# Two-layer decoder trunk on one core: the experts' products from a split operand over 128 tokens to plain fp32 over groups of 32 tokens

## What is computed

```python
def swiglu(xn, w_gu, w_down):
    gate, up = jnp.split(xn @ w_gu, 2, axis=-1)
    return (jax.nn.silu(gate) * up) @ w_down

def moe_swiglu(xn, w_router, w_gu, w_down):
    logits = (xn @ w_router).astype(jnp.float32)
    vals, idx = lax.top_k(logits, TOP_K)
    wts = jax.nn.softmax(vals, axis=-1)
    combine = jnp.sum(jax.nn.one_hot(idx, N_EXPERTS, dtype=jnp.float32) * wts[..., None], axis=-2).astype(xn.dtype)
    out = jnp.zeros_like(xn)
    for e in range(N_EXPERTS):
        out = out + combine[..., e:e + 1] * swiglu(xn, w_gu[e], w_down[e])
    return out
```

## Time and profile before

| | |
|---|---|
| runs | 1526.94, 1527.23, 1527.39 us |
| span of the profiled execution, first to last instruction | 1525.5 us (1.7 under the median; its own time is not listed) |
| TensorE busy | 1492.0 us, 98% |
| VectorE, ScalarE, POOL busy | 1187.4, 986.0, 57.1 us |
| DMA, mean over the span | 299 GB/s, 455.57 MB |
| bytes read from memory | 434.89 MB |

### The profile page before, as it was taken

How to read it: one execution, slowest core, us unless ns; L and a number is a source line. 1 busy time by engine, 2 the same in 40 slices (tenths; PEclk the granted TensorE clock), 3 DMA queues, 4 the chain that set the end, 5 groups by cost and what they waited for, 6 DMA issues and landing times.

```text
span 1525.5 us, 20065 instructions
## 1 busy us (share of the span) xinstructions
PE 1492.0 (98%) x7081; PEld 1214.1 (80%) x7081; DVE 1187.4 (78%) x1047; ACT 986.0 (65%) x1001; POOL 57.1 (4%) x83
## 2 busy tenths in 40 slices
PE   7999999999999989999999999999999999999998
PEld 6888788887776568888888888888888888888886
DVE  1489655545658558898888889889888889888997
ACT  4645444444525527778777778778778778778774
POOL 2000100000111010000000000000000000000100
PEclk9999999999999989999999999999999999999999
DMA  9333585448638039999999999999999999999994
GB/s 363 130 111 111 185 257 180 178 166 220 217 138 290 15 110 374 369 363 386 394 367 377 394 378 363 393 391 355 395 376 362 395 385 357 393 392 356 397 392 169
DMA packets 213026, 455.57 MB, mean 299 GB/s; under 512 B 9857, under 2 KB 36522, under 8 KB 212970
## 3 DMA queue, kind: packets, MB, share of 16 engines
q1 hardware_dynamic: 206624, 441.48, 79.8%
q0 software_dynamic: 3536, 12.96, 2.1%
q10 hardware_dynamic: 2810, 0.40, 0.2%
HBM read 434.89 MB, written 19.92 MB: 298 GB/s over the span
## 4 chain that ended last, share of the span: by engine, by line
PE 94%; DVE 4%; POOL 1%; issue 1%; ACT 0%; DMA 0%; DVEq 0%; POOLq 0%; ACTq 0%
PE bank L2354 60%; PE bank L1947 8%; PE bank L1964 4%; PE bank L1817 4%; PE bank L1858 3%; PE bank L2033 2%; PE bank L2209 2%; PE bank L1839 2%; PE bank L2374 2%; PE bank L1891 1%; PE bank L2103 1%; PE bank L2067 1%; DVE small L1517 1%; PE bank L2151 1%; PE bank L2178 1%
## 5 line engine op out<-in xcount | busy, mean ns | idle before, releaser
L1676 DVE TENSOR_TENSOR w_lo<-ring,w_hi 128x2048 fp32r<-128x2048 f32 x333 | 756.4, 2290 | 104.6 <-ACT w_hi L1027 104.0
L1027 ACT ACTIVATE w_hi<-ring 128x2048 fp32r<-128x2048 f32 x333 | 638.0, 1920 | 168.8 <-PE bank L2354 168.6
L2354 PE MATMUL bank<-w_hi,x_hi 128*128 128x512 f32 x896 | 244.3, 394 | 0.7 <-DVE x_lo L1684 0.7
L2354 PE MATMUL bank<-w_hi,x_lo 128*128 128x512 f32 x896 | 240.0, 390 | 0.0
L2354 PE MATMUL bank<-w_lo,x_hi 128*128 128x512 f32 x896 | 239.7, 389 | 0.0
L2354 PEld LDWEIGHTS bank<-w_hi,x_lo 128*128 128x128 f32 x896 | 168.2, 188 | 35.9
L2354 PEld LDWEIGHTS bank<-w_lo,x_hi 128*128 128x128 f32 x896 | 168.2, 188 | 35.2
L2354 PEld LDWEIGHTS bank<-w_hi,x_hi 128*128 128x128 f32 x896 | 164.5, 188 | 32.3 <-issue 0.9
L1241 DVE TENSOR_TENSOR ring_lo<-ring,f_whi 128x1024 fp32r<-128x1024 f32 x66 | 80.6, 1225 | 75.5 <-ACT f_whi L817 75.5
L2354 PE MATMUL bank<-w_hi,t_hi 128*128 128x512 f32 x448 | 122.6, 395 | 0.0
L2354 PE MATMUL bank<-w_hi,t_lo 128*128 128x512 f32 x448 | 121.1, 392 | 0.0
(11 more groups left out here) (307 smaller groups left out, 1596.6 us busy)
## 6 DMA issues: line engine op xcount, KB each, us to landing
ring<-in_moe_w_gu SPq DMA_DIRECT2D x224, 1024.0 KB, 7.6
ring<-in_moe_w_down SPq DMA_DIRECT2D x112, 1024.0 KB, 8.1
ring<-in_ffn_w_gu SPq DMA_DIRECT2D x22, 1024.0 KB, 8.1
ring<-in_hgrn_w_in SPq DMA_DIRECT2D x16, 1024.0 KB, 15.2
ring<-in_ffn_w_down SPq DMA_DIRECT2D x10, 1024.0 KB, 6.3
x_rows<-arena SPq DMA_DIRECT2D x2, 4096.0 KB, 20.2
ring<-in_kv_w SPq DMA_DIRECT2D x6, 1024.0 KB, 6.3
ring<-in_hgrn_w_out SPq DMA_DIRECT2D x4, 1024.0 KB, 6.3
```

Source lines behind the costliest of these rows:

```text
L1027: act.activation(w_hi[s % PARTS][:, :], raw[:, s % RAWS, :], ACT.Copy).then_inc(hi_ready, 1)
L1676: dve.tensor_tensor(w_lo[s % PARTS][:, :], raw[:, s % RAWS, :], w_hi[s % PARTS][:, :].bitcast(F32), ALU.subtract).then_inc(lo_ready, 1)
L2354: last = mm(out_, x_[k], w[:, k, 512 * b:512 * b + 512], start=start and k == 0 and n == 0, stop=stop and k == HALF // width - 1 and n == 2)
```

## The change

- Experts are computed in plain fp32, without the split: no `w_hi`, `w_lo`, no rounding and no subtraction. A product is one fp32 matmul in place of three fp32r ones.
- Tokens of an expert are cut in groups of 32. The stationary operand is 128 x 32, and four matmuls for the four quarters of the weight columns write the four blocks of 32 partitions of one bank (`block_product`, `row_product`). So a bank holds 32 tokens by 4 x 512 hidden columns.
- Experts are ordered by how many tokens they have. Eight places with 3, 2, 3, 3, 3, 3, 4, 2 groups take them: expert 0 is first, the fullest other is in place 6, the emptiest two in places 7 and 1. A token beyond its place's capacity sets the flag (`most > 0`), and 16 rounds of spill rows, each with a whole expert's weights, would follow.
- Weights come as 46 parts an expert, in phases: gate and up of hidden columns 0 to 2047 (8 + 8 parts, partition p has row 8p + k, 2048 columns, runs of 8 KB), gate and up of the remaining 1536 columns (8 + 8 parts, 6 KB), down (8 + 6 parts of two rows of 1024 values that lie together, 8 KB). There are 14 buffers in place of 7, and a part is free when TensorE has used it.
- The hidden values are transposed by VectorE, in blocks of 32 x 32 (`hidden`), as are the token rows (`turned_rows`). The results go out in rows of 1 KB quarters.
- TensorE, SP, ACT, DVE and POOL have the experts written out, no loop.
- Fewer rows are cleared in memory: 736 for the tokens in place of 2048, and two in place of 1152 for the results.

```diff
-HALF, RAWS, PARTS = ITEM // 2, 7, 3
-NCH = FFE // 512
-PER_E = 3 * NCH
-HALVES = 2 * PER_E
+HALF, RAWS = ITEM // 2, 14
...
+GROUPS = (3, 2, 3, 3, 3, 3, 4, 2)
+RANK = (0, 6, 2, 3, 4, 5, 1, 7)
+LAST = NE - 1
+BEFORE = tuple(sum(GROUPS[:p]) for p in range(NE + 1))
+CAPS = tuple(32 * g for g in GROUPS)
+BASE = tuple(32 * g for g in BEFORE[:NE])
+MAIN = 32 * BEFORE[NE]
+SPILL_G = 3
+SPILL_Y = (6, 7, 0)
+SPILL = T - min(CAPS)
+SPILLS = NE * SPILL // (32 * SPILL_G)
+ZEROS = (BASE[LAST], NE * SPILL)
+WIDE = (512, 384)
+COLS = (0, 4 * WIDE[0])
+DEEP = (WIDE[0] // 32, WIDE[1] // 32)
+PHASES = ((0, 0), (0, 1), (1, 0), (1, 1))
+FIRST = (0, 8, 16, 24, 32, 40)
+N_PART = 46
...
+        def raw(r):
+            at = (ITEM + r * HALF) % (SLOTS * ITEM)
+            return ring[:, at // ITEM, at % ITEM:at % ITEM + HALF]
+        def raw_full(r):
+            return half_full[r // 2] if r % 2 else slot_full[(r // 2 + 1) % SLOTS]
+        def part_here(n):
+            r = n % RAWS
+            before = 0 if r % 2 else 2 * len(range((r // 2 + 1) % SLOTS, I_MOE, SLOTS))
+            return raw_full(r), 16 * (before + n // RAWS + 1)
...
-            def halves_of(e, E, first, last):
-                for s in range(first, last):
-                    (_, kind, c), a = expert_items[s // 2], s % 2
...
-                    sp.dma_start(dst, src).then_inc(raw_full[s % RAWS], 16)
...
+            def weights(dst, s, e):
+                ph, n = phase_of(s)
+                if ph < 4:
+                    c, up = PHASES[ph]
+                    c0 = up * FFE + COLS[c]
+                    src = moe_w_gu[0, bass.ds(e, 1), :, c0:c0 + 4 * WIDE[c]].rearrange("o (p k) c -> p (o k) c", k=KD)
+                    return sp.dma_start(dst[:, 0:4 * WIDE[c]], src[:, n, :])
+                c = ph - 4
+                src = moe_w_down[0, bass.ds(e, 1), COLS[c]:COLS[c] + P * DEEP[c], :].rearrange(
+                    "o (p b) c -> p (o b) c", b=DEEP[c])
...
+            for n in range(NE * N_PART):
+                p, s = divmod(n, N_PART)
+                if s == 0 and p:
+                    if p == 1:
+                        sp.wait_ge(route_ready, 1)
+                    e = sp.value_load(m_exp[0:1, p:p + 1], min_val=0, max_val=NE - 1)
+                if n == 10:
+                    sp.wait_ge(res_ps, 11)
+                if n == 12:
+                    sp.wait_ge(res_ps, 12)
+                if n >= RAWS:
+                    sp.wait_ge(*part_used(n - RAWS))
+                weights(raw(n % RAWS), s, e).then_inc(raw_full(n % RAWS), 16)
...
+            def bring(r0, G):
+                for q in range(4):
+                    pool.dma_start(m_x[32 * q:32 * q + 32, 0:G, :], rows(x_rows, r0, G, q)).then_inc(x_full, 16)
...
-                    act.activation(w_hi[s % PARTS][:, :], raw[:, s % RAWS, :], ACT.Copy).then_inc(hi_ready, 1)
...
+            def gated(g, b, c, made, taken):
+                act.wait_ge(e_ps, made)
+                act.wait_ge(e_h, taken)
+                act.activation(m_sl[:, g, 0:WIDE[c]], bank[:, b, 0:WIDE[c]], ACT.Silu).then_inc(e_sl, 1)
...
-                    dve.tensor_tensor(w_lo[s % PARTS][:, :], raw[:, s % RAWS, :], w_hi[s % PARTS][:, :].bitcast(F32),
-                                      ALU.subtract).then_inc(lo_ready, 1)
...
+            def turned_rows(w, G, came):
+                dve.wait_ge(x_full, came)
+                step(dve.transpose(m_xt[:, w, 0:G, :, :], m_x[:, 0:G, :].rearrange("p g (a b) -> p g b a", b=KD)))
+                dve.tensor_tensor(m_xt[:, w, 0:G, :, :], m_xt[:, w, 0:G, :, :],
+                                  gain[:, G_ROWS:G_ROWS + KD].unsqueeze(1).unsqueeze(3).broadcast_to([P, G, KD, 32]),
+                                  ALU.mult).then_inc(xt_ready, 1)
...
+            def hidden(g, w, b, c, made, gate, turned, done):
+                dve.wait_ge(e_ps, made)
+                dve.wait_ge(e_sl, gate)
+                if turned is not None:
+                    dve.wait_ge(e_t, turned)
+                dve.tensor_tensor(m_h[:, w, 0:WIDE[c]], m_sl[:, g, 0:WIDE[c]], bank[:, b, 0:WIDE[c]],
+                                  ALU.mult).then_inc(e_h, 1)
+                dve.wait_ge(e_h, gate)
+                dve.wait_ge(y_ps, done)
+                dve.transpose(m_t[c][:, g, :, :],
+                              m_h[:, w, 0:WIDE[c]].rearrange("p (a b) -> p b a", b=DEEP[c])).then_inc(e_t, 1)
...
-            def product(dst, s, E, hi, lo, width, start, stop, told=None):
-                pe.wait_ge(hi_ready, E * HALVES + (s + 1))
-                wh, wl = part_of(s, w_hi), part_of(s, w_lo)
-                order = [(k, n, b) for n in range(3) for k in range(HALF // width) for b in range(len(dst))]
-                if told:
-                    order.sort(key=lambda at: at[2])
-                for k, n, b in order:
-                    if (k, n, b) == (0, 2, 0):
-                        pe.wait_ge(lo_ready, E * HALVES + (s + 1))
...
-                    last = mm(out_, x_[k], w[:, k, 512 * b:512 * b + 512],
-                              start=start and k == 0 and n == 0,
-                              stop=stop and k == HALF // width - 1 and n == 2)
...
+            def block_product(b, g, k, w, c, x):
+                for j in range(4):
+                    last = mm(bank[32 * j:32 * j + 32, b, 0:WIDE[c]], m_xt[:, x, g, k, :],
+                              w[:, WIDE[c] * j:WIDE[c] * j + WIDE[c]], start=k == 0, stop=k == KD - 1)
+                return last
...
+            def row_product(y, g, b, w, c):
+                for j in range(4):
+                    last = mm(bank[32 * j:32 * j + 32, y, 0:256], m_t[c][:, g, b, :], w[:, b % 2, 256 * j:256 * j + 256],
+                              start=c == 0 and b == 0, stop=c == 1 and b == DEEP[1] - 1)
+                return last
...
+            def wide(p, ph):
+                c, up = PHASES[ph]
+                for k in range(KD):
+                    if p == 0 and ph == 0:
+                        pe.wait_ge(x_act, k + 1)
+                    w = part_full(N_PART * p + FIRST[ph] + k)
+                    for g in range(GROUPS[p]):
+                        if k == 0 and turns.index((p, ph, g)) >= 8:
+                            pe.wait_ge(*bank_free(p, ph, g))
+                        last = block_product(bank_of(p, ph, g), g, k, w, c, p % 2)
+                        if k == KD - 1:
+                            last.then_inc(e_ps, 1)
+                    if k < KD - 1:
+                        last.then_inc(w_free, 1)
...
+            for p in range(NE):
+                if p:
+                    pe.wait_ge(xt_ready, p)
+                wide(p, 0)
+                if p == LAST:
+                    pe.wait_ge(PW_ready, 1)
+                    pe.wait_ge(*bank_free(LAST, "P turned", 0))
+                    for g in range(2):
+                        for tb in range(TB):
+                            last = tp(bank[:, bank_of(LAST, "P turned", 0), T * g + P * tb:T * g + P * tb + P],
+                                      m_PW[:, tb, g, :, :].rearrange("p j t -> p (j t)"), ident)
+                    last.then_inc(PT_ps, 1)
+                wide(p, 1)
+                wide(p, 2)
+                wide(p, 3)
+                down(p, 0)
+                down(p, 1)
...
-            with pe.If(most > P):
-                all_experts(NE, 1)
...
+            with pe.If(most > 0):```

The streams show where the work went. TensorE's stream within an expert, in the loop's body: `x_hi` and `x_lo` are the tokens' two halves, `xT` in the second fence holds the 32-token groups, `ring` the weight buffers. Before, two parts of gate or up:

```order
L2344 REGISTER_ALU
L2354 MATMUL bank<-w_hi_50,x_hi 128x512 x4
L2354 MATMUL bank<-w_hi_50,x_lo 128x512 x4
L2354 MATMUL bank<-w_lo_53,x_hi 128x512 x4
L2344 REGISTER_ALU
L2354 MATMUL bank<-w_hi_51,x_hi 128x512 x4
L2354 MATMUL bank<-w_hi_51,x_lo 128x512 x4
L2354 MATMUL bank<-w_lo_54,x_hi 128x512 x4
L2372 REGISTER_ALU
L2374 MATMUL bank<-cf,arena 128x128 x4
```

702 lines of the change are left out of this document (338 added, 364 removed).

## The result

The changed kernel takes **1454.37 us**, the median of 4 runs (1451.67 to 1458.12), beside 1527.31 us for the kernel before on the same chip: ratio 0.9524, 95% interval 0.9509 to 0.9538. Run once more, it took 1452.97 us (1450.91 to 1457.46), ratio 0.951 [0.9497, 0.9523]. The forecast was 1443 us in 1405 to 1515: side and range held, and the time itself came 11 us later than forecast.

A forecast was written before the change was run, and what follows sets the result against it. TensorE bounds the kernel, 98% busy, with DMA just as full at 380 GB/s. Start 564.4 + products 834.7 + waits 33 + end 9.4 = 1441.5 us of span, so 1443 us; range 1405 to 1515.

The forecast's parts named there:

- The signs named in advance: Expert stretch: passes 430 and 218 ns apart, DMA above 415 GB/s while TensorE waits, 86 to 90 code packets, VectorE under a quarter busy.
- 430 ns for four passes of 512 columns, 322 for 384, and 218 for 256: TensorE's expert products: quarters run side by side at these times, so a 32-token group costs 36.3 us, 23 groups 834.7.
- Weights of 111.5 us an expert: Slowest DMA engine, per expert: 102.7 us of weight parts, 2.2 of token rows, 6.6 of code.
- Waits: 33 us: TensorE waiting for weights: 7.4 at place 1, 10.4 over places 2 to 5, 5.0 at place 7, plus 10.
- Place 0 uses 2.6 us of that lead: First expert place: of 14 parts ready at the start (34.1 us of transfer), 2.6 us is used, leaving 31.5.
- 77.6 - 72.6 = 5.0: Last place, starting with 14 of 46 parts: 77.6 us of transfers against 72.6 of products, a wait of 5.0 us.
- Start 564.4: Start of the expert products: gather from 560.36 at half clock, then one 0.3 us copy, giving 564.4 us.
- Tail 9.4: After the last matmul: 9.4 us where 8.9 stood, with one more copy and the scatter's smaller matmuls behind VectorE's additions.
- 0.7 us: VectorE's transpose of a 128x512 piece, per group: 0.7 us, between bounds of 0.68 and 2.29, hidden beside other work.
- B: Weight transfers: longer runs bring nothing, rate stays 387 GB/s, 122.6 us an expert, 1528 us (1475 with code spread); chance 0.18.
- C: TensorE's instruction feed: at 54.5 ns an instruction every pass costs 436 ns, 1779 us in all; decides from 39 ns; chance 0.14.
- D: Expert stretch: quarters run in turn, about 3900 us, or router counts miss the places and spill rounds add 1640 us; chance 0.06.

The follow-up runs named there:

- the 20-group kernel: Against the changed kernel, places 0 to 3 take two groups each (2, 2, 2, 2, 3, 3, 4, 2), experts reordered to follow: 1438.89 us, ratio 0.9426.

## Why the prediction was right, and where it was off

The mechanism was right: narrow quarters side by side, DMA close behind, waits mostly in places 1 and 7. The time came 11 us later than forecast. In the span, 10.6 us longer than the sum, TensorE's waits have 12.3 us more, the start 1.3 and the end 0.3; the products took 3.5 us less and hide a part of it, which was luck. The signs named in advance came too: quads 429 and 216 ns apart, 421 GB/s from 725 to 765 us while TensorE waits for each part, 89 packets of code, VectorE busy for a tenth of the experts' time.

- **"430 ns for four passes of 512 columns, 322 for 384, and 218 for 256"**: 429, 322 and 216. A group costs 36.1 us in place of 36.3, so 23 groups 831.2 in place of 834.7 us. The four blocks of L2119 and the pairs of L2067 did carry over to a long stream with all 128 rows in use.
- **"Weights of 111.5 us an expert"**: right as a sum, with two terms off in opposite directions. Transfers are 30 x 2.49 + 16 x 1.88 = 104.8 us in place of 102.7 (2.49 / 8 is 311 ns for a packet of 8 KB and 1.88 / 8 is 235 for one of 6 KB, where 304 and 231 were read off a line through 2 and 4 KB), and code is at most 11 x 0.18 = 2.0 us in place of 6.6. With 2.2 for rows that makes 109.0 at most, against the 108.7 to 109.7 of the 20-group kernel. Places 2 to 5 of the kernel after last 111.2 on average, more than either the transfers or their 108.4 us of products; no run takes that apart. The count of code packets was right: 111 less 22 is 89, for 88.
- **"Waits: 33 us"**: this term failed; they are 45.3. Places 2 to 5 wait 11.0 where I had 10.4, and 1.8 are the half clock at the start. The rest is the lead. First, **"Place 0 uses 2.6 us of that lead"** was wrong. The queue's row of place 0 shows 39.05 MB of the 44.04 MB that it consumes:

```profile
q1 hardware_dynamic: 5927, 39.05, 91.2%
```

  So 5.0 MB of the lead were still under way at its end, 12 us at 412 GB/s. The size of the parts did it, as the run with equal pieces shows: DMA idled while small parts replaced large ones and couldn't follow afterwards. The windows of the kernel after:

```profile
568.00:590.00 22.00, 22.00 (x204) 6.16 (x200) 1.20 (x5) 2.24 (x5) 2.27 (x4) 0.97 0.88 319
590.00:610.00 20.00, 20.00 (x196) 5.64 (x188) 2.67 (x4) 0.00 (x0) 0.00 (x0) 1.00 0.90 310
...
640.00:676.00 36.00, 36.00 (x676) 20.00 (x672) 2.73 (x5) 0.61 (x2) 0.00 (x0) 1.00 1.01 419
```

  With 109.0 us of transfers in 72.3 us of products, place 1 was short of 36.7; a lead of 34.1 - 12.1 = 22 us leaves 14.7 of them, and 19.1 were measured. The queue's row from 675.95 to 767.3, place 1's time, has the rest:

```profile
q1 hardware_dynamic: 5611, 36.65, 98.5%
```

  Of the 14.7 MB of lead 9.7 were there at its start, and 9.7 + 36.65 is 2.3 MB more than the 44.04 that it consumes: the first part of place 2 and pieces of those behind it, 5.6 us at 412 GB/s in which nothing came that place 1 could use. This loss at the end of a lead is what I had added 10 us for. Booked there, place 1 comes out 1.7 us too low.
  The larger miss is place 7, **"77.6 - 72.6 = 5.0"**, which waited 13.4. The view of its time, 1356.57 to 1442.4, and of its first 10 us:

```profile
DMA packets 5592, 33.55 MB, mean 391 GB/s; under 512 B 672, under 2 KB 672, under 8 KB 3360
...
q1 hardware_dynamic: 4812, 30.77, 88.1%
...
1356.00:1366.00 10.00, 10.00 (x104) 3.17 (x100) 0.00 (x0) 1.11 (x3) 2.19 (x4) 1.00 0.95 360
```

  The ring held 13.3 MB at its start and not 14.7, for place 6 gives buffers back slowly to its end (305 GB/s from 1320 to 1356). Beside the 30.77 MB of weights 2.8 MB of rows and code moved, 6.7 us at 412 GB/s. All 33.55 MB are 81.4 us at that rate, 9.1 over the products; the last part's products, which can't begin before it has landed (1.9 us), the four transposes (0.6) and the slow first 10 us (1.3) make it 12.9 of the 13.4. Of all this my 77.6 us had only the rows and the code, with 6.1.
- **"Start 564.4"**: the first product starts at 565.71. The gather began at 557.86, 2.5 us earlier than before, but its 32 passes took 7.9 us for 5.6, all at half clock (0.50 from 560 to 566, where the earlier trace rows has 0.50 only until 564); the first four quads of place 0 still started 855 ns apart. **"Tail 9.4"**: 9.7 us from the last products to the span's end (1442.4 to 1452.1).
- **"0.7 us" for a transpose of VectorE** was too low: 1.05 us for 128x512 (0.96 is the mean of both sizes), nearer to its lower bound than to the upper 2.29. It hides all the same, as does every other cover: VectorE is busy 34.47 us of 335 in the places' middle stretch.
- With the measured terms the sum is 565.7 + 831.2 + 45.3 + 9.7 = 1451.9 us of span, for 1452.1 measured. This only shows that nothing is left over, since 45.3 is itself what the products leave.

The rivals. *B* (longer runs bring nothing) is refuted by the run with 2 KB runs: 389 GB/s against 411, 31 us. The rate itself fell between B's and mine, nearer to mine: a 1 MB part in 2.49 us is 421 GB/s, where 2.435 us had meant 431 and B had 387. *C* (TensorE can't be fed) did not come: down's stretch above holds 672 passes and 672 loads in 36.43 us, 27 ns each, without a gap, where C needed more than 39. *D* was wrong in both halves: the quarters run side by side, and the spill rounds were not entered (the weights' queue moved 337.66 MB from 564 to 1443 us, which is the 352.3 MB of all experts less the 14.7 of the lead).

The Trainium skill's 358 GB/s a core (HBM Reference, Specifications), by which the kernel would have taken about 1600 us by the prediction's estimate, is passed by the 412 of this trace; the 425 that the page gives to a core that streams alone fit with the 421. Its 62 ns a matmul under software decoding (TensorE: Matmul & The Clock Gate, Part 2) is not a floor here: a pass with its load takes 54.

## What to carry to other kernels

When two engines of near equal pace are coupled by a ring, work out the waits place by place with the lead as it is after the first stage, and not as it was loaded: a ring counts buffers, not bytes, so where large parts follow small ones the lead melts before it is spent (5.0 of 14.7 MB here). What is still in flight when a lead ends is lost too (2.3 MB), and a stage that empties the ring at the program's end also waits for what other queues move beside it and for its last part. Once the transfers set the pace, taking work off the other engine gives little (three groups, 108 us of TensorE, gave 14), while the length of a run still gives (2 KB to 8 KB, 31 us of 1486). With few tokens a row of 32-wide column quarters in plain fp32 is a real choice against a split operand over 128, but only as long as padding stays low: 23 groups gain 73 us, 30 lose 147.
